# Sparse attention: softmax weights transposed as a rounded part and a rest

## The chip, the cores and the metric

The kernel runs on one NeuronCore of a Trainium2 chip. The metric is the device time of one execution in microseconds. The kernel before was run three times: 3642.68, 3643.70 and 3645.34 us, median 3643.7.

## The reference, cut to what matters

The model has two blocks. In its second layer stands a sparse attention over 16 + 512 tokens with 16 heads; a query attends to a chosen set of latent key rows:

```python
def block(qa, qi, wi, qpos):
    ...                       # index scores, the best keys of each query
    logits = (jnp.einsum("bqhr,bqkr->bqhk", qa, kv).astype(jnp.float32) * B_KV_RANK ** -0.5
              + jnp.swapaxes(bias, -1, -2))
    p = jax.nn.softmax(jnp.where(valid[:, :, None, :], logits, NEG_INF), axis=-1)
    o_lat = jnp.einsum("bqhk,bqkr->bqhr", p.astype(kv.dtype), kv)
    o = jnp.einsum("bqhr,hrd->bqhd", o_lat, w_uv)
```

All is float32. The change touches how the weights p get from query rows to key rows between the softmax and the product with the values.

## The kernel before

The program is one long chain of stages on one core, written engine by engine with semaphores; nothing is scheduled by a tool, so the order on each engine is the order in the code. The feed-forward stages (`fa_`, `fb_`, `fd_`, `ff_`) fill most of the time. Their matmuls are of type float32r, a reduced float32: an operand is written as a rounded part (`xh`, `wh`) and the rest (`xl`, `wl`), and three products are summed in PSUM (L371, L430). The sparse attention computes with plain float32 matmuls; the profile shows each of them as two records.

`dsa_stage` runs `latents` (projections, norms) and then `latent_heads`, the place of the change. `latent_heads` first makes the queries of all heads (L1602, weights fetched in three slots), their norms, and the index scores with the choice of keys on DVE. Then comes the head loop. A step g is one head `hd` and one query tile `t` of four, with 144, 272, 400 and 528 visible keys; there are 16 * 4 = 64 steps.

- PE: `turn(g)` (L1643) transposes the weights of step g, first the 16 meta keys (L1652, the data as a 128x16 stationary operand, the identity as 128 moving columns), then t + 1 blocks of 128x128 (L1654); `scores(g + 4)` (L1638) computes logits four steps ahead, since each tile has its own PSUM bank; `outputs(hd - 1)` (L1662, L1664) follows in the step t = 0. The last step of a head also waits for `mixed`, since its meta block goes to the bank of the outputs.
- DVE: `logit(g)` scales and adds the bias from PSUM (L1817), adds the mask and takes the maximum (L1820); then `weigh(g - 1)` takes the reciprocal of the denominator (L1827) and multiplies (L1829), in place in `b_work`.
- ACT: `spread(g)` copies the turned blocks to SBUF (L1745, L1748), then `exps(g + 3)` (L1735); `store` copies a head's output to `b_mix` (L1753).
- SP fetches: behind the last norm sum (L1576) it issues the first two of eight output weights (L1580), the others each behind a finished output product (L1698).

The buffers: `b_work` (`early`) holds queries, scratch and, later, logits and turned weights; the tile `b_vals` holds the values, and `l_q_all` the queries of all heads.

Of the kernel before, what the change touches and what calls it, by code (L numbers as in the profile page):

```python
# [15 lines left out]
P = 128  # L16
# [48 lines left out]
        "q_mm q_ev squared added_sq ssq_mm i_mm relued i_added v_mm v_ev u_mean u_root scored logits expd "  # L65
# [27 lines left out]
def build(nc, x_t, meta_t, mem_t, bias_onehot, dil_onehot, rel_bias, dil_table, gains, wi, wo, w_out,  # L93
# [3 lines left out]
    with top:  # L97
# [1211 lines left out]
        EARLY = IDX_COLS + 4 * TOK + 6 * SEQ + 2 * SEQ + 3 * 2 * RANK  # L1309

        def early_parts(early):

            at, parts = 0, []
            for cols, shape, names in ((4 * SEQ, "p (c t) -> p c t", {"c": 4}), (TOK, None, {}),
                                       (4 * TOK, "p (s t) -> p s t", {"s": 4}),
                                       (4 * SEQ, "p (s r t) -> p s r t", {"s": 2, "r": 2}),
                                       (2 * SEQ, "p (s t) -> p s t", {"s": 2}), (2 * SEQ, "p (k t) -> p k t", {"k": 2}),
                                       (6 * RANK, "p (s n) -> p s n", {"s": 3})):
                part = early[:, at:at + cols]
                parts.append(part.rearrange(shape, **names) if shape else part)  # L1320
                at += cols
            return parts

        def dsa_stage():
            with ExitStack() as st:
                mix = sb(st, "b_mix", [P, KC, SEQ])
                bw = sb(st, "b_bw", [P, HEADS, TOK])
                ckv = sb(st, "b_ckv", [P, 2, TOK])
                vals = sb(st, "b_vals", [P, QT, B_HEADS * 64])
                valm = sb(st, "b_valm", [META, B_HEADS * 64])  # L1330
                mb = sb(st, "b_mb", [P, QT, TOK])
                g_lat = sb(st, "b_g_lat", [P, 3, 2])
                early = sb(st, "b_work", [P, EARLY])
                widx = sb(st, "b_widx", [P, QT, IDX_HEADS])
                eps_q = sb(st, "b_eps_q", [P, QT])
                uv = mix[:, 0:4, :].rearrange("p k t -> p (k t)").rearrange("p (h n) -> p h n", h=B_HEADS)
                c_bw, uq0, uq1, uq2, uv_there = sems(st, "b_")
                uq_there = [uq0, uq1, uq2]
                with ExitStack() as s2:
                    latents(s2, ckv, g_lat, widx, eps_q, uv, bw, c_bw, early, uq_there, uv_there)  # L1340
                with ExitStack() as s2:
                    latent_heads(s2, ckv, vals, valm, g_lat, widx, eps_q, mb, mix, uv, bw, c_bw, early, uq_there, uv_there)

        def latents(st, ckv, g_lat, widx, eps_q, uv, bw, c_bw, early, uq_there, uv_there):
# [13 lines left out]
            qidx, kidx, _, _, _, qn, w_uq = early_parts(early)  # L1358
# [161 lines left out]
        def latent_heads(st, ckv, vals, valm, g_lat, widx, eps_q, mb, mix, uv, bw, c_bw, early, uq_there, uv_there):  # L1520

            q_all = sb(st, "l_q_all", [P, 2 * B_HEADS, SEQ])
            top8 = sb(st, "l_top8", [P, 8])
# [5 lines left out]
            qidx, kidx, act_r, sq, sq_sum, qn, w_uq = early_parts(early)  # L1529
# [4 lines left out]
            WO_AT = EARLY - 2 * KC * P  # L1534
            pt = early[:, PT_AT:PTM_AT].rearrange("p (u j q) -> p u j q", u=2, j=QT)
            ptm = early[:, PTM_AT:PTM_AT + 2 * SEQ].rearrange("p (u q) -> p u q", u=2)
            w_o = early[:, WO_AT:EARLY].rearrange("p (s n) -> p s n", s=2)
            (q_mm, q_ev, squared, added_sq, ssq_mm, i_mm, relued, i_added, v_mm, v_ev, u_mean, u_root, scored, logits,
# [31 lines left out]
            with nc.Block() as block:  # L1570
                @block.sync
                def _(sp):
                    for hd in range(3, B_HEADS):
                        sp.wait_ge(q_mm, 1 + hd - 2)
                        sp.dma_start(w_uq[:, hd % 3, :], b_uq[hd]).then_inc(uq_there[hd % 3], 16)
                    sp.wait_ge(ssq_mm, 1 + B_HEADS)  # L1576
                    for c in range(KC):
                        if c >= 2:
                            sp.wait_ge(o_mm, 1 + c - 1)
                        sp.dma_start(w_o[:, c % 2, :], w_out[1, c]).then_inc(wo_there[c % 2], 16)  # L1580
                    fetch_first(sp, 3)

                @block.gpsimd
                def _(pool):
                    for hd in range(B_HEADS):
# [8 lines left out]
                def _(pe):  # L1594
# [48 lines left out]
                    def turn(g):  # L1643
# [6 lines left out]
                        pd, bank = lg_of(g), T_BANK[g % 2]  # L1650
                        to = acc[0:META, bank, (t + 1) * P:(t + 2) * P] if t < NT - 1 else acc[0:META, O_BANK, 0:P]
                        pe.transpose(to, pd[:, 0:META], ident[:, :])  # L1652
                        for j in range(t + 1):
                            last = pe.transpose(acc[:, bank, j * P:(j + 1) * P], pd[:, META + j * P:META + (j + 1) * P],  # L1654
                                                ident[:, :])
# [26 lines left out]
                    pe.wait_ge(v_ev, 1 + len(v_jobs))  # L1682
                    for g in range(LAST):
# [92 lines left out]
                def _(dve):  # L1776
# [46 lines left out]
                    def weigh(g):  # L1823
                        lg = lg_of(g)
                        s = g % 8
                        dve.wait_ge(expd, 1 + g + 1)
                        dve.reciprocal(rden[:, s:s + 1], den[:, s:s + 1])  # L1827
                        dve.drain()
                        dve.tensor_scalar(lg, lg, rden[:, s:s + 1], None, ALU.mult).then_inc(weights, 1)  # L1829
# [1473 lines left out]
```

## Time and profile before

| | |
|---|---|
| median of three runs | 3643.7 us |
| profiled execution, its own time | 3643.14 us |
| its span | 3641.3 us, 51388 instructions |
| granted TensorE clock, mean | 0.984 of 2.4 GHz |
| PE busy | 3518.0 us (97%) |
| DVE busy | 1752.5 us (48%) |
| ACT busy | 1329.3 us (37%) |
| head loop, first to last turn | 1715.6 to 1866.8 us of the span |

How to read it: a busy PE means that some matmul record is open, not that the array is at its peak; successive records overlap, so the time that a matmul takes in a stream is the distance between two starts, not its length. PEld is the load of the stationary operand. Where the view merges records ("x3"), the length runs from the first start to the last end. The granted clock is 1.00 for 2.4 GHz and 0.50 for 1.2 GHz.

### The profile page before, as it was taken

The numbers are of one execution on the slowest core, as the hardware profiler recorded it, in microseconds if no ns is written. First come the engines' busy times: TensorE is split into PE (matmuls) and PEld (weight loads), VectorE is DVE, ScalarE is ACT, GpSimd is POOL, SyncE is SP. The second block draws the span as 40 slices with busy tenths as digits, with TensorE's granted clock in tenths as the row PEclk, the third lists the DMA queues.
The fourth block names the chain that finished last, engine by engine and source line by source line (L and its number), as shares of the span: only waits on it lengthen the run. The fifth ranks groups of instructions, "written<-read, shape, count | busy, mean of one in ns | idle before, by whom it ended". The sixth has DMA issues, their size and how long they took to land. (4 is left out here: it accounts for less than half of the span.)

```text
span 3641.3 us, 51388 instructions
## 1 busy us (share of the span) xinstructions
PE 3518.0 (97%) x20338; PEld 2956.1 (81%) x20338; DVE 1752.5 (48%) x2511; ACT 1329.3 (37%) x1840; POOL 596.1 (16%) x656
## 2 busy tenths in 40 slices
PE   8999999999999999988999999999989999899998
PEld 7999977799999999754547888888866677678886
DVE  5443377554434443266635443544269633554433
ACT  4332366443323332134524332333231244334421
POOL 0000122200000000011005755540032323320000
PEclk9999999899999999989999999999999999999999
DMA  5322411032222222300003223332234421322222
GB/s 171 136 85 88 142 52 48 21 108 86 81 88 106 82 89 83 136 24 27 1 29 110 101 108 121 130 117 86 87 128 142 148 64 53 132 100 104 94 93 79
DMA packets 124082, 334.91 MB, mean 92 GB/s; under 512 B 15192, under 2 KB 58456, under 8 KB 107957
## 3 DMA queue, kind: packets, MB, share of 16 engines
q1 hardware_dynamic: 120884, 324.90, 25.9%
q0 software_dynamic: 3072, 8.39, 0.6%
q8 instruction: 72, 1.18, 0.1%
q14 instruction: 54, 0.43, 0.0%
HBM read 316.36 MB, written 25.40 MB: 94 GB/s over the span
## 5 line engine op out<-in xcount | busy, mean ns | idle before, releaser
L371 PE MATMUL acc<-fb_xh,fb_wh 128*128 128x264 f32 x1408 | 287.7, 285 | 3.2 <-DVE fb_wl L550 3.2
L371 PE MATMUL acc<-fb_xl,fb_wh 128*128 128x264 f32 x1408 | 288.0, 286 | 0.0
L371 PE MATMUL acc<-fb_xh,fb_wl 128*128 128x264 f32 x1408 | 287.5, 286 | 0.0
L371 PE MATMUL acc<-fd_xh,fd_wh 128*128 128x512 f32 x704 | 275.4, 391 | 3.2 <-DVE fd_wl L550 3.2
L371 PE MATMUL acc<-fd_xl,fd_wh 128*128 128x512 f32 x704 | 274.4, 390 | 0.0
L371 PE MATMUL acc<-fd_xh,fd_wl 128*128 128x512 f32 x704 | 274.4, 390 | 0.0
L446 ACT ACTIVATE fb_wh<-fb_raw 128x2048 fp32r<-128x2048 f32 (+1 forms) x74 | 124.7, 1686 | 286.9 <-PE acc L430 173.8
L371 PEld LDWEIGHTS acc<-fb_xh,fb_wh 128*128 128x128 f32 x1408 | 219.9, 189 | 3.6 <-DVE fb_wl L550 3.5
L371 PEld LDWEIGHTS acc<-fb_xl,fb_wh 128*128 128x128 f32 x1408 | 219.2, 189 | 0.0
L371 PEld LDWEIGHTS acc<-fb_xh,fb_wl 128*128 128x128 f32 x1408 | 218.7, 189 | 0.0
L545 DVE TENSOR_TENSOR fb_wl<-fb_raw,fb_wh 128x2048 fp32r<-128x2048 f32 (+1 forms) x74 | 148.3, 2004 | 141.2 <-ACT fb_wh L446 140.3
L446 ACT ACTIVATE fd_wh<-fd_raw 128x2048 fp32r<-128x2048 f32 (+1 forms) x74 | 124.8, 1686 | 248.2 <-PE acc L430 158.0
L545 DVE TENSOR_TENSOR fd_wl<-fd_raw,fd_wh 128x2048 fp32r<-128x2048 f32 (+1 forms) x74 | 152.3, 2058 | 130.5 <-ACT fd_wh L446 129.4
L446 ACT ACT_TABLE_LOAD x60 | 77.0, 1283 | 298.8 <-PE acc L371 298.7
L1589 POOL TENSOR_TENSOR b_work<-b_work 128x512 f32<-128x512 f32 x16 | 20.7, 1295 | 949.5 <-ACT b_work L1717 949.5
L784 POOL TENSOR_TENSOR fa_wl<-fa_raw,fa_wh 128x1024 fp32r<-128x1024 f32 x30 | 71.1, 2375 | 633.0 <-ACT fa_wh L1026 633.0
L371 PEld LDWEIGHTS acc<-fd_xh,fd_wh 128*128 128x128 f32 x704 | 132.5, 188 | 31.7 <-DVE fd_wl L550 4.0
L371 PEld LDWEIGHTS acc<-fd_xl,fd_wh 128*128 128x128 f32 x704 | 132.5, 188 | 28.1 <-issue 0.5
L371 PEld LDWEIGHTS acc<-fd_xh,fd_wl 128*128 128x128 f32 x704 | 132.4, 188 | 27.7
L371 PE MATMUL acc<-fa_xh,fa_wh 128*128 128x264 f32 x704 | 144.3, 286 | 7.3 <-DVE fa_wl L550 7.3
L642 DVE SCALAR_TENSOR_TENSOR h<-acc,h 128x264 f32<-128x264 f32 (+1 forms) x72 | 35.1, 516 | 230.9 <-PE acc L430 230.9
L371 PE MATMUL acc<-fa_xl,fa_wh 128*128 128x264 f32 x704 | 144.4, 286 | 0.0
(555 smaller groups left out, 9141.1 us busy)
## 6 DMA issues: line engine op xcount, KB each, us to landing
fb_raw<-wi_dram SPq DMA_DIRECT2D x42, 1024.0 KB, 4.7
fd_raw<-wi_dram SPq DMA_DIRECT2D x42, 1024.0 KB, 4.8
fb_raw<-wo_dram SPq DMA_DIRECT2D x32, 704.0 KB, 4.0
fd_raw<-wo_dram SPq DMA_DIRECT2D x32, 704.0 KB, 4.1
fa_raw<-wi_dram SPq DMA_DIRECT2D x20, 1024.0 KB, 4.7
ff_raw<-wi_dram SPq DMA_DIRECT2D x20, 1024.0 KB, 4.7
fa_raw<-a_qkv_dram SPq DMA_DIRECT2D x24, 512.0 KB, 4.1
m_raw<-gate_w_dram SPq DMA_DIRECT2D x24, 512.0 KB, 3.4
```

The costliest lines, as they stand in the source:

```text
L371: last = pe.matmul(acc[:, up_base(p, b) + 2 * a + q, 0:w], x[:, k, a, :], part[:, k, t0:t0 + w], start=k == 0 and part is xh and x is wv, ...
L446: act.activation(wh[:, b, 0:n_], raw[:, b, 0:n_], ACT.Copy).then_inc(rounded, 1)
L545: dve.tensor_tensor(wl[:, b, 0:n_], raw[:, b, 0:n_], wh[:, b, 0:n_].bitcast(F32), ALU.subtract).then_inc(split, 1)
L642: last = dve.scalar_tensor_tensor(hv, acc[:, down_base(p) + 2 * (c % 2) + q, 0:w], 0.5, hv, ALU.mult, ALU.add)
L784: pool.tensor_tensor(wl[:, c % RING, :], raw[:, c % RING, :], wh[:, c % RING, :].bitcast(F32), ALU.subtract).then_inc(split, 1)
L1589: pool.tensor_tensor(sq_sum[:, hd % 2, :], sq[:, hd % 2, 0, :], sq[:, hd % 2, 1, :], ALU.add).then_inc(added_sq, 1)
```

## The change

`turn` no longer uses the transposing form on float32 data. `weigh` now writes two float32r tiles, `hi` (the product, rounded by its output type) and `lo` (the product again, less `hi`), into a new buffer `l_pd` with two slots, g mod 2. `turn` multiplies each block twice by an identity of type float32r, once for each part, and the bank sums them. POOL makes this identity once. Since `l_pd` has two slots, `weigh(g)` waits until `turn(g - 2)` is done. To make room, `early` gets smaller: the normed query latents move to `b_vals`, the three slots of query weights to `b_mix`, and the output weights to the first four planes of `l_q_all`, so that their loads wait until the scores of heads 0 and 1 are computed.

```diff
-        EARLY = IDX_COLS + 4 * TOK + 6 * SEQ + 2 * SEQ + 3 * 2 * RANK
+        EARLY = 2 * sum(keys for _, _, keys, _ in REAL_TILES) + 2 * QT * SEQ + 2 * SEQ
...
+                qn = vals[:, 0, :].rearrange("p (k t) -> p k t", k=2)
+                w_uq = mix[:, 4:7, :]
...
+            ident_r = sb(st, "l_ident", [P, P], F32R)
...
+            pd = sb(st, "l_pd", [P, 2, 2, TOK], F32R)
...
-            w_o = early[:, WO_AT:EARLY].rearrange("p (s n) -> p s n", s=2)
+            w_o = q_all[:, 0:4, :].rearrange("p c t -> p (c t)").rearrange("p (s n) -> p s n", s=2)
...
-                    sp.wait_ge(ssq_mm, 1 + B_HEADS)
+                    sp.wait_ge(scored, 1 + 2 * NT)
...
+                    pool.tensor_copy(ident_r[:, :], ident[:, :]).then_inc(ident_on, 1)
...
-                        pd, bank = lg_of(g), T_BANK[g % 2]
+                        bank, keys = T_BANK[g % 2], WIDTHS[t]
                         to = acc[0:META, bank, (t + 1) * P:(t + 2) * P] if t < NT - 1 else acc[0:META, O_BANK, 0:P]
-                        pe.transpose(to, pd[:, 0:META], ident[:, :])
+                        for r in range(2):
+                            pe.matmul(to, pd[:, g % 2, r, 0:META], ident_r[:, :], start=r == 0, stop=r == 1)
                         for j in range(t + 1):
-                            last = pe.transpose(acc[:, bank, j * P:(j + 1) * P], pd[:, META + j * P:META + (j + 1) * P],
-                                                ident[:, :])
+                            for r in range(2):
+                                last = pe.matmul(acc[:, bank, j * P:(j + 1) * P],
+                                                 pd[:, g % 2, r, META + j * P:META + (j + 1) * P], ident_r[:, :],
+                                                 start=r == 0, stop=r == 1)
                         last.then_inc(turned, 1)
...
+                    pe.wait_ge(ident_on, 2)
...
+                        hi, lo = (pd[:, g % 2, r, 0:WIDTHS[STEPS_[g][1]]] for r in range(2))
                         dve.reciprocal(rden[:, s:s + 1], den[:, s:s + 1])
                         dve.drain()
-                        dve.tensor_scalar(lg, lg, rden[:, s:s + 1], None, ALU.mult).then_inc(weights, 1)
+                        if g >= 2:
+                            dve.wait_ge(turned, 1 + g - 1)
+                        dve.tensor_scalar(hi, lg, rden[:, s:s + 1], None, ALU.mult)
+                        dve.drain()
+                        dve.scalar_tensor_tensor(lo, lg, rden[:, s:s + 1], hi.bitcast(F32), ALU.mult,
+                                                 ALU.subtract).then_inc(weights, 1)
```

On PE, in the head loop from the last three steps of one head into the next, the order before (each row is line, operation, output and inputs, output size and count):

```order
L1652 MATMUL acc<-ident,b_work 16x128
L1654 MATMUL acc<-ident,b_work 128x128 x2
L1638 MATMUL acc<-b_ckv,l_q_all 128x272 x2
L1652 MATMUL acc<-ident,b_work 16x128
L1654 MATMUL acc<-ident,b_work 128x128 x3
L1638 MATMUL acc<-b_ckv,l_q_all 128x400 x2
L1652 MATMUL acc<-ident,b_work 16x128
L1654 MATMUL acc<-ident,b_work 128x128 x4
L1638 MATMUL acc<-b_ckv,l_q_all 128x512 x2
```

And the same place now (turns are L1656 and L1659, scores L1641):

```order
L1656 MATMUL acc<-l_ident,l_pd 16x128 x2
L1659 MATMUL acc<-l_ident,l_pd 128x128 x4
L1641 MATMUL acc<-b_ckv,l_q_all 128x272 x2
L1656 MATMUL acc<-l_ident,l_pd 16x128 x2
L1659 MATMUL acc<-l_ident,l_pd 128x128 x6
L1641 MATMUL acc<-b_ckv,l_q_all 128x400 x2
L1656 MATMUL acc<-l_ident,l_pd 16x128 x2
L1659 MATMUL acc<-l_ident,l_pd 128x128 x8
L1641 MATMUL acc<-b_ckv,l_q_all 128x512 x2
```

Nothing changes place on PE; each turning instruction became two.

On DVE, at the start of the head loop (steps 0 and 1), before:

```order
L1827 RECIPROCAL l_rden<-l_den 128x1
L1829 TENSOR_SCALAR b_work<-b_work,l_rden 128x144
L1817 SCALAR_TENSOR_TENSOR b_work<-acc,l_rq,b_bw 128x400
L1820 ISA b_work,l_nmx<-b_work,b_mb 128x400
L1820 ISA l_nmx 128x1
L1827 RECIPROCAL l_rden<-l_den 128x1
L1829 TENSOR_SCALAR b_work<-b_work,l_rden 128x272
```

And now (logits are L1824 and L1827, the weights L1835 to L1841):

```order
L1835 RECIPROCAL l_rden<-l_den 128x1
L1839 TENSOR_SCALAR l_pd<-b_work,l_rden 128x144
L1841 SCALAR_TENSOR_TENSOR l_pd<-b_work,l_rden,l_pd 128x144
L1824 SCALAR_TENSOR_TENSOR b_work<-acc,l_rq,b_bw 128x400
L1827 ISA b_work,l_nmx<-b_work,b_mb 128x400
L1827 ISA l_nmx 128x1
L1835 RECIPROCAL l_rden<-l_den 128x1
L1839 TENSOR_SCALAR l_pd<-b_work,l_rden 128x272
L1841 SCALAR_TENSOR_TENSOR l_pd<-b_work,l_rden,l_pd 128x272
```

One operation per step is added behind the multiplication, and the next logit stands behind it.

## Rows read from the trace of the kernel before

**Rows 1.** Page, part 1: busy time of each engine and share of the span.

```profile
PE 3518.0 (97%) x20338; PEld 2956.1 (81%) x20338; DVE 1752.5 (48%) x2511; ACT 1329.3 (37%) x1840; POOL 596.1 (16%) x656
```

**Rows 2.** Windows around the head loop: busy us, granted clock, DMA share, GB/s.

```profile
1715.60:1719.00 3.40, 3.24 (x12) 2.69 (x13) 3.02 (x10) 1.25 (x5) 0.00 (x0) 0.50 0.02 5
...
1780.00:1820.00 40.00, 40.00 (x181) 22.92 (x180) 25.34 (x84) 22.35 (x73) 0.00 (x0) 1.00 0.00 1
```

**Rows 3.** Timeline, PE: start us, length us, engine, line; one head apart.

```profile
1794.05 1.07 PE L1662 MATMUL acc<-b_work,b_valm 16*64 16x512 f32 x2
...
1803.81 1.07 PE L1662 MATMUL acc<-b_work,b_valm 16*64 16x512 f32 x2
```

**Rows 4.** Timeline, PE: one turn of three full blocks.

```profile
1798.59 0.27 PE L1652 MATMUL acc<-ident,b_work 128*16 128x128 f32 x1
1798.70 0.49 PE L1654 MATMUL acc<-ident,b_work 128*128 128x128 f32 x3
1799.03 1.51 PE L1638 MATMUL acc<-b_ckv,l_q_all 128*128 128x400 f32 x4
```

**Rows 5.** Timeline: records of few columns behind full weight loads.

```profile
1690.32 1.03 PE L1609 MATMUL acc<-ones,b_work 128*128 128x1 f32 x8
...
1792.88 0.41 PEld L1638 LDWEIGHTS acc<-b_ckv,l_q_all 128*128 128x128 f32 x3 [0.24 <-issue]
```

**Rows 6.** Timeline, PE: float32r matmuls of 264 and of 512 columns.

```profile
1200.39 0.41 PE L371 MATMUL acc<-fb_xh,fb_wh 128*128 128x264 f32 x2
1200.63 0.41 PE L371 MATMUL acc<-fb_xl,fb_wh 128*128 128x264 f32 x2
...
2299.87 0.39 PE L371 MATMUL acc<-fd_xh,fd_wh 128*128 128x512 f32 x1
...
2300.10 0.39 PE L371 MATMUL acc<-fd_xl,fd_wh 128*128 128x512 f32 x1
```

**Rows 7.** One line's instructions: float32r weight loads, ns min/median/max.

```profile
L371 PEld LDWEIGHTS acc<-fb_xh,fb_wh x1408: 187/188/333, 738.3 to 1386.1; 128*128 128x128 f32 x176
```

**Rows 8.** Groups by form, PE: the float32r matmul of fewest columns.

```profile
L2495 PE MATMUL acc<-d_mh,m_wh 128*128 128x256 f32 x64 | 18.6, 290 | 0.0
```

**Rows 9.** Timeline, PE: the two records of a float32 matmul of 128 columns.

```profile
1797.03 0.38 PE L1664 MATMUL acc<-b_work,b_vals 128*64 128x128 f32 x2
```

**Rows 10.** Timeline, DVE: logit steps at the loop's start, unbroken until 1722.10.

```profile
1715.40 0.63 DVE L1817 SCALAR_TENSOR_TENSOR b_work<-acc,l_rq,b_bw 128x400 f32<-128x400 f32 x1
...
1722.50 0.63 DVE L1817 SCALAR_TENSOR_TENSOR b_work<-acc,l_rq,b_bw 128x400 f32<-128x400 f32 x1 [0.40 <-PE acc L1638]
```

**Rows 11.** Groups by form, DVE: times of one; the three-operand form in SBUF.

```profile
L1829 DVE TENSOR_SCALAR b_work<-b_work,l_rden 128x528 f32<-128x528 f32 x16 | 7.9, 496 | 1.2
...
L1192 DVE SCALAR_TENSOR_TENSOR a_pd<-a_lg,a_rden,a_pd 128x528 f32<-128x528 f32 x8 | 6.1, 768 | 0.7
...
L1192 DVE SCALAR_TENSOR_TENSOR a_pd<-a_lg,a_rden,a_pd 128x400 f32<-128x400 f32 x8 | 5.1, 635 | 0.7
...
L1192 DVE SCALAR_TENSOR_TENSOR a_pd<-a_lg,a_rden,a_pd 128x272 f32<-128x272 f32 x8 | 4.0, 502 | 0.7 <-issue 0.2
...
L1192 DVE SCALAR_TENSOR_TENSOR a_pd<-a_lg,a_rden,a_pd 128x144 f32<-128x144 f32 x8 | 3.0, 370 | 0.6
```

**Rows 12.** Waits in the head loop: us in total, times, longest.

```profile
DVE b_work L1817 <- PE acc L1638: 41.0, 44, 1.8
```

**Rows 13.** Timeline: first and second turn of the loop, and the last.

```profile
1715.64 0.37 PE L1652 MATMUL acc<-ident,b_work 128*16 128x128 f32 x1 [3.17 <-DVE b_work L1829]
...
1717.30 0.09 PEld L1652 LDWEIGHTS acc<-ident,b_work 128*16 128x16 f32 x1 [0.47 <-DVE b_work L1829]
...
1866.85 0.27 PE L1652 MATMUL acc<-ident,b_work 128*16 128x128 f32 x1 [0.75 <-ACT b_mix L1753]
```

**Rows 14.** One line's instructions: the loads of the output weights.

```profile
L1580 SPq DMA_DIRECT2D b_work<-w_out_dram x8: 327/328/434, 1691.4 to 1913.2; - x8
...
DMA to landing us min/median/max: 3.3/3.5/4.3
```

More of the change, by code:

```diff
@@ L64 @@
     "l_": (
-        "q_mm q_ev squared added_sq ssq_mm i_mm relued i_added v_mm v_ev u_mean u_root scored logits expd "
+        "ident_on q_mm q_ev squared added_sq ssq_mm i_mm relued i_added v_mm v_ev u_mean u_root scored logits expd "
         "weights turned pt_ready pv_mm mixed wo0 wo1 o_mm o_added"),
@@ L1316, in early_parts @@
                                        (4 * SEQ, "p (s r t) -> p s r t", {"s": 2, "r": 2}),
-                                       (2 * SEQ, "p (s t) -> p s t", {"s": 2}), (2 * SEQ, "p (k t) -> p k t", {"k": 2}),
-                                       (6 * RANK, "p (s n) -> p s n", {"s": 3})):
+                                       (2 * SEQ, "p (s t) -> p s t", {"s": 2})):
                 part = early[:, at:at + cols]
@@ L1339, in dsa_stage, with latents @@
                 with ExitStack() as s2:
-                    latents(s2, ckv, g_lat, widx, eps_q, uv, bw, c_bw, early, uq_there, uv_there)
+                    latents(s2, ckv, g_lat, widx, eps_q, uv, qn, w_uq, bw, c_bw, early, uq_there, uv_there)
                 with ExitStack() as s2:
-                    latent_heads(s2, ckv, vals, valm, g_lat, widx, eps_q, mb, mix, uv, bw, c_bw, early, uq_there, uv_there)
-        def latents(st, ckv, g_lat, widx, eps_q, uv, bw, c_bw, early, uq_there, uv_there):
+                    latent_heads(s2, ckv, vals, valm, g_lat, widx, eps_q, mb, mix, uv, qn, w_uq, bw, c_bw, early, uq_there, uv_there)
+        def latents(st, ckv, g_lat, widx, eps_q, uv, qn, w_uq, bw, c_bw, early, uq_there, uv_there):
             xn = sb(st, "b_xn", [P, KC, TOK])
@@ L1357, in latents @@
             s_q = sb(st, "b_s_q", [P, QT])
-            qidx, kidx, _, _, _, qn, w_uq = early_parts(early)
+            qidx, kidx, _, _, _ = early_parts(early)
             (there_g, there_i, there_cq, there_kv, there_q, sq_a, sq_d, summed, rooted, normed, idx_mm, cq_mm,
@@ L1518, in _, with latent_heads @@
                     last.then_inc(ckv_on, 1)
-        def latent_heads(st, ckv, vals, valm, g_lat, widx, eps_q, mb, mix, uv, bw, c_bw, early, uq_there, uv_there):
+        def latent_heads(st, ckv, vals, valm, g_lat, widx, eps_q, mb, mix, uv, qn, w_uq, bw, c_bw, early, uq_there, uv_there):
             q_all = sb(st, "l_q_all", [P, 2 * B_HEADS, SEQ])
+            ident_r = sb(st, "l_ident", [P, P], F32R)
             top8 = sb(st, "l_top8", [P, 8])
@@ L1528, in latent_heads @@
             rden = sb(st, "l_rden", [P, 8])
-            qidx, kidx, act_r, sq, sq_sum, qn, w_uq = early_parts(early)
+            qidx, kidx, act_r, sq, sq_sum = early_parts(early)
+            pd = sb(st, "l_pd", [P, 2, 2, TOK], F32R)
             WIDTHS = [keys for _, _, keys, _ in REAL_TILES]
@@ L1533, in latent_heads @@
             PTM_AT = PT_AT + 2 * QT * SEQ
-            WO_AT = EARLY - 2 * KC * P
             pt = early[:, PT_AT:PTM_AT].rearrange("p (u j q) -> p u j q", u=2, j=QT)
             ptm = early[:, PTM_AT:PTM_AT + 2 * SEQ].rearrange("p (u q) -> p u q", u=2)
-            w_o = early[:, WO_AT:EARLY].rearrange("p (s n) -> p s n", s=2)
-            (q_mm, q_ev, squared, added_sq, ssq_mm, i_mm, relued, i_added, v_mm, v_ev, u_mean, u_root, scored, logits,
+            w_o = q_all[:, 0:4, :].rearrange("p c t -> p (c t)").rearrange("p (s n) -> p s n", s=2)
+            (ident_on, q_mm, q_ev, squared, added_sq, ssq_mm, i_mm, relued, i_added, v_mm, v_ev, u_mean, u_root, scored, logits,
              expd, weights, turned, pt_ready, pv_mm, mixed, wo0, wo1, o_mm, o_added) = sems(st, "l_")
```

## The prediction

> **What bounds the kernel now.** I read the busy shares first: PE is busy for 97% of the span, DVE for 48% [rows 1]. That says little of one stage, so I then read the windows around the head loop, where the change acts: in its steady part PE is busy for 40.00 of 40 us at full clock, DVE for 25.3, ACT for 22.4, and hardly a byte moves [rows 2]. Then two starts of the same matmul one head apart: 1794.05 and 1803.81, so a head takes 9.76 us [rows 3]. DVE waits for the scores of PE for 41.0 us in 44 places of the loop [rows 12]. PE sets the pace, and what is added to PE's stream in the loop is added to the time, as long as DVE keeps up.
>
> In a stream the price of a matmul is the distance between starts. In a turn of one meta block and three full blocks the starts are 1798.59, 1798.70 and, for what follows, 1799.03: 0.11 for the meta block and 0.33 / 3 = 0.11 for each full one [rows 4]. A turn of tile t has t + 2 such intervals, the last reaching to the next instruction's first record. A head has 2 + 3 + 4 + 5 = 14, so 1.54 of its 9.76 us are turning.
>
> **What sets 0.11 us.** It could be 128 columns streaming at two cycles each, or the load of the next 128 stationary columns. The trace tells them apart. Eight norm-sum records stream a single column each behind a full load, and take 1.03 us together: at most 0.13 each [rows 5]. Three loads for score records of 16 columns span 0.41 us, with 0.19 as one's own length [rows 5, 7], so they start (0.41 - 0.19) / 2 = 0.11 apart. So one full float32 load per 0.11 us is the floor, whatever streams behind it. The trace has no float32r load that is dense enough to show its floor: with 264 columns the starts are 0.24 us apart for two, 0.12 each, and with 512 columns 0.23 [rows 6]. Two things follow from these: float32r streams one column per cycle (0.107 and 0.213 us at 2.4 GHz), with some 0.013 us on top. The load's own length is 187 to 188 ns in float32r [rows 7], which is also what the loads in rows 5 show. I take the floor to be the same, 0.11.
>
> **The change part by part, PE.** Each turn has twice the instructions, with a load each. The intervals of the new turn: from the first meta pass to the second, where the next load has only 16 columns, so that the streaming decides: 128 / 2.4 = 0.053 us and the 0.013, 0.066; from there 2(t + 1) intervals that each end in a full load, 0.11; and the last one to the scores' load, 0.11 as before. Over a head: 4 * 0.066 + 20 * 0.11 + 4 * 0.11 = 2.90 us against 1.54, which is 1.36 more. Sixteen heads: 21.8 us. Bounds of the one unseen price, the interval of a full float32r load behind a pass of 128 columns: from above 0.22 us, two float32 records of 128 columns, which start 0.38 - 0.27 = 0.11 apart [rows 4, 9]; from below 0.053 us, the streaming alone. I take 0.11, since the nearest rows, those with few columns, lie there. With 0.1225 as in rows 6 the loop would take 4 us more, and with 0.11 for the meta pass 2.8 more.
>
> **DVE.** The new operation reads SBUF and has three operands. The same form took 370, 502, 635 and 768 ns at these widths, and the drain ahead of it costs as L1829's idle, 1.2 us in 16 or 0.075 [rows 11]. Per head: 2.28 + 0.30 = 2.58 us. DVE's present need per head I read where it does not wait: from 1715.40 to 1722.50 - 0.40 = 1722.10 it does four steps, one of each width, in 6.70 us [rows 10]. So it will need 9.3 us against PE's 9.76 + 1.36 = 11.1. If the multiplication with a float32r output fell to the pace of the three-operand form (768 instead of 496 ns at the widest, at most 0.27 in each step), 10.4. Covered in both cases; the cover is 0.7 to 1.8 us per head, and beyond it each microsecond costs 16.
>
> **The new wait.** `weigh(g)` waits for `turn(g - 2)`, and behind it on DVE stand `logit(g + 2)` and all else. From the end of `turn(g - 2)` to the start of `turn(g)` PE has two blocks of scores and a turn to do; the 400-column block alone lasts 1.51 us [rows 4], and the multiplication with the rest needs at most 0.50 + 0.08 + 0.77 = 1.35. No wait for PE comes of it in the steady part. ACT's work is as before, and its share is the smallest of the three.
>
> **Start and end of the loop.** The first turn waits 3.17 us for the first weights, and the second turn's load waits again for DVE [rows 13]. There DVE is on the path: up to the second turn come 0.37 + 0.08 and 0.50 + 0.08, 1.0 us, of which the sum above holds 0.2 for the first turn. The clock stands at 0.50 there [rows 2]; if it stays so over the next two turns, their added passes, 0.29 + 0.40 us, take about twice that. Together 1.5 us. At the end the last turn waits for ACT's store for 0.75 us [rows 13], which hides a part of the passes added just before it, and the last weights come 0.85 later; I count nothing.
>
> **The rest.** POOL copies 128x128 once, long before it is needed: nothing. The first two output weights are issued some 30 us later than at 1691.4, and land in 3.5 us [rows 14], still over 140 us before they are used. Query weights and latents only move. Nothing.
>
> The sum: 21.8 + 1.5 = 23.3 us on the profiled execution's 3643.14 gives 3666.4; the median of the runs lies 0.6 above it, so 3667.0.
>
> **The rivals.** First, the load of a float32r block is shorter than 0.11 and hides under the pass. Then 24 intervals per head fall to 0.066 and four stay: 1.58 + 0.44 = 2.02, 0.48 more than now, 7.7 us in sixteen heads, with the start 9.2: 3653. For it speaks that no row shows a dense float32r load; against it that its length is the float32 one. If then the multiplication fell to the slower pace, DVE's 10.4 would bind over PE's 10.2, 3 us more. The Trainium skill ("TensorE: Matmul & The Clock Gate", Weight-path perf modes — Fast Weight Load (FWL) and DoubleRow) says that fast weight load is on for 128 weights if the input type is not FP32, and measured about twice the speed. Whether float32r counts as FP32 the page does not say; by that rule, if it does not, the load would be some 54 ns as an estimate from that page and the time this rival's. Rows 7, where a float32r load lasts as long as a float32 one, speak against it.
>
> Second, on the other side, not slower: the transposing form costs two cycles a column, as many as two float32r passes of one cycle each, and neither loads nor the 0.013 us count. All 28 intervals are 0.053: 1.49 instead of 1.54, which gives back 0.8 us and leaves the start's 1.5: 3644. It decides from a mean interval of (1.54 + 5.8 / 16) / 28 = 0.068 us downward, since a measurement of this kernel can tell about 0.2%, 7.3 us, from no change. It needs the one-column records of rows 5 to be an exception.
>
> Third, a float32r pass under 256 columns costs as much as the float32 matmul of its size, two records, 0.22 us. The float32r matmul of fewest columns in the trace has 256 [rows 8], so no row excludes it; against it stands that float32r matmuls show one record each [rows 6]. Then 28 * 0.22 = 6.16 against 1.54, 4.6 per head, 74 and 1.5: 3719.
>
> Fourth, DVE binds, by slower writes of the new type than any bound above: at 12 us per head 36 + 1.5, 3681.
>
> **How the numbers follow.** The forecast gets 0.72, its own range 3664 to 3675 (0.053 for the meta pass at one end, 0.1225 and 0.11 at the other). The first rival 0.10, the second 0.04, the third 0.11, the fourth 0.03. The range must take in the first rival and the fourth: 3652 to 3682, which leaves out the second and the third. Slower by over 0.2%: forecast, third, fourth and nearly all of the first, 0.94; same 0.05; faster 0.01.
>
> **What would show it.** Starts of the output matmul one head apart: 11.1 us if I am right, 10.2 for the first rival, 9.7 for the second, 14.4 for the third. Starts of full turning passes 0.11 apart, each with its load; the distance of the two meta passes near 0.066. PE still busy for 40 of 40 us, DVE for about 30 of 40 and waiting for scores less than now. The new operation at 768 ns for 528 columns, and the multiplication near 496. I am wrong if the distance of the full passes is not near 0.11, or if PE has gaps in the loop that end at DVE's weights.

## The result and the profile after

The changed kernel takes 3671.3 us (median of four runs, 3670.94 to 3673.33) against 3644.5 us of the kernel before. The ratio of the runs is 1.0078, 95% interval 1.0065 to 1.0090. Over five more runs, with the kernel before beside them, it was 1.0072 (1.0058 to 1.0085): slower by 26 to 28 us, where 23.3 were forecast.

First the page of the changed kernel, its span and its busy shares:

```profile
span 3669.7 us, 51967 instructions
PE 3545.9 (97%) x20562; PEld 2981.7 (81%) x20562; DVE 1789.5 (49%) x2575; ACT 1329.4 (36%) x1840; POOL 592.8 (16%) x657
```

The shares are those of [rows 1] to a point, and tell nothing of the stage. The windows do (columns as in [rows 2]: PE, PEld, DVE, ACT and POOL busy us, granted clock, DMA share, GB/s). Steady loop, its start, and what follows its end:

```profile
1719.00:1722.00 3.00, 2.63 (x12) 2.25 (x12) 2.73 (x9) 1.06 (x5) 0.00 (x0) 0.50 0.02 5
...
1780.00:1820.00 40.00, 40.00 (x211) 25.34 (x210) 30.02 (x87) 19.29 (x63) 0.00 (x0) 1.00 0.00 1
...
1894.00:1896.00 2.00, 2.00 (x5) 0.74 (x5) 0.00 (x0) 0.00 (x0) 0.00 (x0) 0.72 0.00 0
1896.00:1898.00 2.00, 2.00 (x7) 0.87 (x5) 0.00 (x0) 0.02 (x1) 0.00 (x0) 0.50 0.00 0
```

PE is busy for 40.00 of 40 us as before, DVE for 30.0 where it was 25.3, which is 8.4 us of a head's 11.15. At the start the clock is 0.50, as in [rows 2]. In the last pair, behind the last turn, the clock stands at 0.72 and 0.50, where the trace of before has 1.00.

Next the timeline of PE across one head, which answers to [rows 3]:

```profile
1797.00 1.07 PE L1668 MATMUL acc<-b_work,b_valm 16*64 16x512 f32 x2
...
1803.72 0.59 PE L1656 MATMUL acc<-l_ident,l_pd 128*16 128x128 f32 x2
1804.15 1.05 PE L1659 MATMUL acc<-l_ident,l_pd 128*128 128x128 f32 x8
...
1807.18 0.28 PE L1656 MATMUL acc<-l_ident,l_pd 128*16 128x128 f32 x2
1807.29 0.38 PE L1659 MATMUL acc<-l_ident,l_pd 128*128 128x128 f32 x2
...
1808.15 1.07 PE L1668 MATMUL acc<-b_work,b_valm 16*64 16x512 f32 x2
```

From one output product to the next it is 1808.15 - 1797.00 = 11.15 us; it was 9.76, and 11.1 was forecast. Eight full passes span 1.05 us and two span 0.38, so the starts are (1.05 - 0.38) / 6 = 0.112 us apart. (In two of four turns, as at 1803.72, the record of the first meta pass starts already 0.03 us behind the start of the last scores record, so its own start can't be read there.) Another turn shows the meta passes and what follows, answering to [rows 4]:

```profile
1800.30 0.29 PE L1656 MATMUL acc<-l_ident,l_pd 128*16 128x128 f32 x2
...
1800.43 0.61 PE L1659 MATMUL acc<-l_ident,l_pd 128*128 128x128 f32 x4
...
1802.64 1.56 PE L1641 MATMUL acc<-b_ckv,l_q_all 128*128 128x400 f32 x4
```

From the first meta pass to the first full pass it is 0.13 us for two intervals; over the loop the median from the second meta pass to the first full one is 0.060, near the forecast 0.066. But the first full pass also starts within 0.06 to 0.07 us of the pass before it and not 0.11. On the other side the four records of the scores behind a turn span 1.56 us where they spanned 1.51 [rows 4]: what the start of a turn gains is given back at its end, 0.05 us each, four times in a head. Both belong to one and the same thing, the price of a full load, which shows one record late. The first scores record behind the turn is 551 ns long and those behind it 499, and the surplus of 0.052 is the load's 0.112 less the 0.060 that the last pass streams. So a full pass and the scores behind a turn each cost 0.112 and only the second meta pass 0.060: 24 * 0.112 + 4 * 0.060 = 2.93 us in a head against 1.54, which is 1.39 more. The kernel with half the columns, below, tells this from a cost of changing the type.

DVE's new operation and its multiplication, by form (times as in [rows 11]):

```profile
L1841 DVE SCALAR_TENSOR_TENSOR l_pd<-b_work,l_rden,l_pd 128x528 fp32r<-128x528 f32 x16 | 12.3, 769 | 1.2
...
L1839 DVE TENSOR_SCALAR l_pd<-b_work,l_rden 128x528 fp32r<-128x528 f32 x16 | 7.9, 495 | 17.1 <-PE acc L1659 17.1
```

They take 769 and 495 ns for 528 columns, as the same forms in the rows before, so the float32r output costs nothing. DVE's waits in the loop:

```profile
DVE l_pd L1839 <- PE acc L1659: 17.1, 15, 1.4
...
DVE b_work L1824 <- PE acc L1641: 9.6, 14, 0.7
```

It waits for scores for 9.6 us instead of 41.0 [rows 12], and for the turn two steps back for 17.1. Both are waits of an engine that is ahead. The start and the end of the loop, which answer to [rows 13]:

```profile
1718.24 0.37 PE L1656 MATMUL acc<-l_ident,l_pd 128*16 128x128 f32 x2 [3.61 <-DVE l_pd L1841]
...
1891.10 0.29 PE L1656 MATMUL acc<-l_ident,l_pd 128*16 128x128 f32 x2 [0.64 <-DVE l_pd L1841]
...
1893.12 1.07 PE L1668 MATMUL acc<-b_work,b_valm 16*64 16x512 f32 x2 [0.83 <-ACT b_work L1755]
```

The first turn waits 3.61 us instead of 3.17, 0.44 more for the first rest. The last turn now waits for DVE's rest and no longer for ACT's store, 0.64 us instead of 0.75, and the output product behind it waits 0.83 us for ACT. The loads of the output weights, as in [rows 14]:

```profile
L1582 SPq DMA_DIRECT2D l_q_all<-w_out_dram x8: 327/328/434, 1729.3 to 1939.6; - x8
DMA to landing us min/median/max: 3.4/3.5/4.5
```

The first is issued 38 us later and lands 165 us before its use at 1897.9.

**A ledger of the stage.** The table takes starts of the same matmuls in both traces. The values' matmuls, the last ahead of the loop, end their starts at 1711.9 and 1714.0:

```profile
L1627 PE MATMUL acc<-b_mix,b_ckv x40: 592/592/1061, 1691.3 to 1711.9; 128*128 128x512 f32 x32, 128*16 128x512 f32 x8
```

```profile
L1630 PE MATMUL acc<-b_mix,b_ckv x40: 592/592/697, 1696.8 to 1714.0; 128*128 128x512 f32 x32, 128*16 128x512 f32 x8
```

| stretch | before, us | after, us | more | forecast |
|---|---|---|---|---|
| last matmul of the values to the first output product (turns 0 to 4) | 13.8 | 16.1 | 2.3 | 3.0 |
| first to last output product (turns 5 to 63) | 142.7 | 163.0 | 20.3 | 20.3 |
| last output product to the first matmul with the output weights | 3.3 | 4.8 | 1.5 | 0 |
| from there to the next stage | 58.4 | 58.6 | 0.2 | 0 |
| sum | 218.2 | 242.5 | 24.3 | 23.3 |

The profiled executions differ by more, 3671.51 - 3643.14 = 28.4 us. What lies outside the ledger is asked by the first experiment and by the second trace of the changed kernel. Taken off the spans, the ledger leaves 3423.1 and 3424.7 us in the first two traces of before, and 3427.3 and 3422.9 in the two of the changed kernel.

### The profile page after: what moved, and what is told of

The parts are those of the page before. It is cut to its first block and busy times, and to the rows that moved or that the text cites. A ratio compares the mean times of both kernels' runs of the same rounds, so it can differ in the third digit from the quotient of the medians.

```text
span 3669.7 us, 51967 instructions
## 1 busy us (share of the span) xinstructions
PE 3545.9 (97%) x20562; PEld 2981.7 (81%) x20562; DVE 1789.5 (49%) x2575; ACT 1329.4 (36%) x1840; POOL 592.8 (16%) x657
## 5 line engine op out<-in xcount | busy, mean ns | idle before, releaser
L371 PEld LDWEIGHTS acc<-fb_xl,fb_wh 128*128 128x128 f32 x1408 | 218.5, 188 | 0.0
L371 PE MATMUL acc<-fa_xh,fa_wl 128*128 128x264 f32 x704 | 144.0, 286 | 0.0
```

The source lines that it names most:

```text
L371: last = pe.matmul(acc[:, up_base(p, b) + 2 * a + q, 0:w], x[:, k, a, :], part[:, k, t0:t0 + w], start=k == 0 and part is xh and x is wv, ...
```

## The experiments

**The kernel before once more.**

> The kernel before once more, for a second trace of it. The trace of the changed kernel stands 4.7 us later than that of before already ahead of the sparse attention (first matmul of the feed-forward stage before it at 743.0 against 738.3), in code that the change doesn't touch, and the values of the sparse attention took 3.3 us less. Theory (these are differences from one execution to the next): this trace differs from the first one of the same kernel by some us in those same stages, with the head loop at 9.76 us per head as before. Rival (they come with the changed program): the stages stand within 0.5 us of the first trace. Ratio to before 1.000 in both.

There was no edit. The ratio is 0.9999 (0.9989 to 1.0009). One line's instructions, the first matmuls of the feed-forward stage ahead of the attention (first and last start behind the comma), in the first trace of before, in this one, in that of the changed kernel, and in that of the one-pass kernel below:

```profile
L371 PE MATMUL acc<-fb_xh,fb_wh x1408: 279/285/587, 738.3 to 1386.3; 128*128 128x264 f32 x176
```

```profile
L371 PE MATMUL acc<-fb_xh,fb_wh x1408: 279/285/479, 741.4 to 1389.3; 128*128 128x264 f32 x176
```

```profile
L371 PE MATMUL acc<-fb_xh,fb_wh x1408: 279/285/479, 743.0 to 1390.9; 128*128 128x264 f32 x176
```

```profile
L371 PE MATMUL acc<-fb_xh,fb_wh x1408: 279/285/479, 734.8 to 1382.8; 128*128 128x264 f32 x176
```

The same code starts anywhere from 734.8 to 743.0 us, and the same program differs by 3.1 between two executions. The theory holds: offsets ahead of the attention are no effect of the change. The loop stood at 9.76 us per head, and the ledger's sum at 218.7. Within it two stretches differ. Up to the first output product it is 12.7 us and not 13.8, since the clock rose again 3.0 us behind the first turn instead of 5.7. And from the last output product to the output weights it is 4.9 us and not 3.3, at a low clock:

```profile
1868.00:1870.00 2.00, 2.00 (x5) 0.33 (x4) 0.00 (x0) 0.00 (x0) 0.00 (x0) 0.84 0.00 0
1870.00:1872.00 2.00, 2.00 (x5) 0.90 (x4) 0.00 (x0) 0.00 (x0) 0.00 (x0) 0.50 0.00 0
```

The question that this raises is taken up at the end.

**The layout alone.**

> The change's layout alone: latents, query weights and output weights moved, their loads later, the identity copied by POOL, but one float32 transposing pass per block and the weights in place as before. Theory (the layout costs nothing): 3644, ratio 1.000, head 9.76 us. Rival (the moved buffers or the later loads cost a part of the 28 us between the two profiled executions that the head loop doesn't explain, about 4 us): 3648, ratio 1.001.

```diff
-                        for r in range(2):
-                            pe.matmul(to, pd[:, g % 2, r, 0:META], ident_r[:, :], start=r == 0, stop=r == 1)
+                        pe.transpose(to, lg_[:, 0:META], ident[:, :])
...
-                        dve.tensor_scalar(hi, lg, rden[:, s:s + 1], None, ALU.mult)
...
+                        dve.tensor_scalar(lg, lg, rden[:, s:s + 1], None, ALU.mult).then_inc(weights, 1)
```

Median 3644.19, ratio 1.0004 (0.9995 to 1.0014), ledger's sum 218.2 as before. The layout costs nothing that can be measured.

**DVE's part alone.**

> DVE does all the work of the changed kernel and waits for the turn two steps back, but PE turns only the rounded part, in the transposing form as before; the rest is left out of the output. Theory (all of the loop's cost is PE's passes, DVE and its new wait cost only at the start of the loop): head 9.76 us, about 1 us over the layout alone, 3645. Rival (DVE's longer step and its wait hold PE up): head over 9.9 us, 3 us or more over the layout alone, and PE idle in the loop behind DVE's weights.

```diff
-                        for r in range(2):
-                            pe.matmul(to, pd[:, g % 2, r, 0:META], ident_r[:, :], start=r == 0, stop=r == 1)
+                        hi_ = pd[:, g % 2, 0, :].bitcast(F32)
+                        pe.transpose(to, hi_[:, 0:META], ident[:, :])
```

(The full blocks likewise.) Median 3644.79, ratio 1.0004 (0.9994 to 1.0013); the ledger's sum is 219.7, 1.5 more than before: 1.2 at the start, and 0.25 in the last head, where the last turn waits 0.99 us for DVE's rest instead of 0.75 for ACT. Two output products one head apart on PE's timeline:

```profile
1786.51 1.07 PE L1666 MATMUL acc<-b_work,b_valm 16*64 16x512 f32 x2
...
1796.27 1.07 PE L1666 MATMUL acc<-b_work,b_valm 16*64 16x512 f32 x2
```

9.76 us: DVE's longer step and its wait for the turn two steps back cost nothing in the steady loop. The rival falls. Behind the last turn the clock stays up:

```profile
1872.00:1874.00 2.00, 2.00 (x8) 0.88 (x7) 0.00 (x0) 0.00 (x0) 0.00 (x0) 1.00 0.00 0
```

**One float32r pass.**

> The changed kernel with one float32r pass per block, that of the rounded part; the rest is computed by DVE but left out of the output. Theory (a full weight load sets 0.11 us per full pass in float32r as in the transposing form, and only the meta pass is shorter): head 9.62 us (1.40 instead of 1.54 us of turning), 3644. Rival (the stream of the pass sets it, 0.066 us, and the second pass costs 0.11 only since something else goes with a pair): head 9.34 us, 3639.

```diff
-                        for r in range(2):
-                            pe.matmul(to, pd[:, g % 2, r, 0:META], ident_r[:, :], start=r == 0, stop=r == 1)
+                        for r in range(1):
+                            pe.matmul(to, pd[:, g % 2, r, 0:META], ident_r[:, :], start=r == 0, stop=True)
```

Median 3647.63 where 3644 was expected, ratio 1.0017 (1.0007 to 1.0026). PE's timeline over one head:

```profile
1790.42 1.07 PE L1668 MATMUL acc<-b_work,b_valm 16*64 16x512 f32 x2
...
1796.83 0.61 PE L1659 MATMUL acc<-l_ident,l_pd 128*128 128x128 f32 x4
...
1799.46 0.28 PE L1659 MATMUL acc<-l_ident,l_pd 128*128 128x128 f32 x1
...
1800.21 1.07 PE L1668 MATMUL acc<-b_work,b_valm 16*64 16x512 f32 x2
```

A head takes 9.79 us, neither the 9.62 of the theory nor the 9.34 of the rival. The interval of full passes is (0.61 - 0.28) / 3 = 0.11, as the theory says; what its 9.62 missed is that behind the single meta pass comes a full load, so no interval is short and all 14 cost 0.112, 1.57 us instead of 1.54. The second pass then costs 11.15 - 9.79 = 1.36 us per head, and that is four times 0.060 and ten times 0.112. So the loop's cost is the number of passes, and nothing that goes with a pair.

The stage is 5.0 us longer than in the kernel with the same DVE work and the transposing form (224.6 against 219.7), though the loop is only 0.03 us per head longer; the medians of the two kernels differ by 2.8, of times that spread over 8 to 10 us. The ledger shows where: 16.5 us up to the first output product (15.1 there), 6.0 us behind the last (3.3 there). The windows behind the last turn:

```profile
1867.00:1869.00 2.00, 2.00 (x3) 0.46 (x2) 0.00 (x0) 0.00 (x0) 0.00 (x0) 0.50 0.00 0
1869.00:1871.00 2.00, 2.00 (x6) 0.92 (x4) 0.00 (x0) 0.00 (x0) 0.00 (x0) 0.50 0.00 0
```

The clock is at 0.50 in both, and at 0.63 and 0.67 in the windows next to them; there the output product runs at half speed. The two programs differ only in the form of the turning passes, but their traces also in the moment at which the loop ends; which of the two counts is asked at the end.

**Half the columns, and half the load.**

> The changed kernel, but each full turning pass streams only 64 of its 128 identity columns; loads are as they were, and half of each turned block is left out of the output. Theory (the load of 128 stationary columns sets the interval): full passes stay 0.11 us apart and a head 11.15 us, time as the changed kernel. Rival (streaming sets it): the intervals between full passes, 16 per head, fall by 0.027 to 0.055 us, a head to 10.7 or less, 7 us or more off the time.

```diff
-                                last = pe.matmul(acc[:, bank, j * P:(j + 1) * P],
-                                                 pd[:, g % 2, r, META + j * P:META + (j + 1) * P], ident_r[:, :],
+                                last = pe.matmul(acc[:, bank, j * P:j * P + 64],
+                                                 pd[:, g % 2, r, META + j * P:META + (j + 1) * P], ident_r[:, 0:64],
```

Median 3673.68, ratio 1.0084 (1.0067 to 1.0101), that of the changed kernel or more. PE over one head:

```profile
1794.76 1.07 PE L1668 MATMUL acc<-b_work,b_valm 16*64 16x512 f32 x2
...
1800.36 1.59 PE L1641 MATMUL acc<-b_ckv,l_q_all 128*128 128x400 f32 x4
...
1801.90 1.03 PE L1659 MATMUL acc<-l_ident,l_pd 128*128 128x64 f32 x8
...
1805.05 0.35 PE L1659 MATMUL acc<-l_ident,l_pd 128*128 128x64 f32 x2
...
1805.90 1.07 PE L1668 MATMUL acc<-b_work,b_valm 16*64 16x512 f32 x2
```

> The changed kernel, but each full turning pass loads only 64 stationary columns and writes 64 rows; it streams 128 columns as before, and half of each turned block is left out of the output. Theory (the load sets the interval, at 0.11 us per 128 columns): with half the load the stream of 0.066 us decides, 16 intervals per head fall by 0.046 us, a head to 10.4 us, 12 us off the time of the changed kernel. Rival (each float32r pass of 128 columns costs 0.11 us whatever is loaded): head 11.15 us, no gain.

```diff
-                                last = pe.matmul(acc[:, bank, j * P:(j + 1) * P],
-                                                 pd[:, g % 2, r, META + j * P:META + (j + 1) * P], ident_r[:, :],
+                                last = pe.matmul(acc[0:64, bank, j * P:(j + 1) * P],
+                                                 pd[:, g % 2, r, META + j * P:META + j * P + 64], ident_r[:, :],
```

Median 3655.48, ratio 1.0029 (1.0017 to 1.0040). PE over one head:

```profile
1788.31 1.07 PE L1668 MATMUL acc<-b_work,b_valm 16*64 16x512 f32 x2
...
1793.42 1.56 PE L1641 MATMUL acc<-b_ckv,l_q_all 128*128 128x400 f32 x4
...
1794.94 0.65 PE L1659 MATMUL acc<-l_ident,l_pd 128*64 128x128 f32 x8
...
1797.68 0.28 PE L1659 MATMUL acc<-l_ident,l_pd 128*64 128x128 f32 x2
...
1798.44 1.07 PE L1668 MATMUL acc<-b_work,b_valm 16*64 16x512 f32 x2
```

With half the columns to stream the full passes stay (1.03 - 0.35) / 6 = 0.113 us apart and a head takes 11.14 us. With half the columns to load they are (0.65 - 0.28) / 6 = 0.062 apart and a head takes 10.13. So in a full float32r pass the load of 128 stationary columns sets the pace, 0.112 us, and the stream of 128 moving columns hides in it; with 64 to load the stream sets it, 0.062. The 20 full passes of a head fall by 0.051 each, 1.02 us, which is the whole difference to 11.15; I had expected 16 intervals to fall by 0.046.

The scores behind a turn, four records of 400 columns, show where the surplus of 0.05 us comes from. They span 1.51 us behind transposing passes, 1.56 behind float32r passes of 128 columns (with 128 or 64 columns loaded), and 1.59 behind those of 64 columns. The change of type is the same in the last three, so it does not set the surplus. What does, by this reading, is the scores' own load of 0.112 us less what the last pass covers of it: 0.060 with 128 columns, and some 0.03 with 64 (half of it, an estimate), which leaves 0.05 and 0.08.

The half-column kernel's loop is the changed kernel's, yet its ledger's sum is 248.7, 6.2 more. That lies at the ends: 20.9 us up to the first output product instead of 16.1, 6.2 behind the last instead of 4.8. Its windows from the first turn on, first and last of five in a row:

```profile
1711.00:1714.00 3.00, 2.42 (x12) 2.11 (x13) 2.73 (x8) 1.03 (x4) 0.00 (x0) 0.50 0.02 5
...
1723.00:1726.00 3.00, 3.00 (x4) 1.04 (x4) 0.64 (x2) 1.13 (x4) 0.00 (x0) 0.50 0.00 0
```

All five stand at 0.50, 15 us in all, and the clock rises only in the window behind them (0.81); in the changed kernel the window from 1724 to 1726, 6 us behind its first turn, is back at 0.95. Why it stays low longer here the runs do not show.

**The start of the loop.** Both traces show PE idle ahead of the first turn and then turning at the low clock. ACT loads its exponential table only behind the last eviction of the values, and the first exponential only then; in the trace of before:

```profile
1712.51 0.60 ACT L1730 ACTIVATE b_vals<-acc 128x512 f32<-128x512 f32 x1 [1.12 <-PE acc L1627]
1713.12 1.28 ACT L1735 ACT_TABLE_LOAD   x1
```

> The kernel before, with the first three exponentials of the head loop issued by ACT among the evictions of the values (behind the fifth, seventh and ninth) instead of behind them all. Theory (PE's idle 3.2 us ahead of the first turn comes from ACT's table load and first exponential behind the evictions, and the granted clock of 0.5 after it from that idle time): the first turn follows the values' last eviction at once, the clock stays at 1.0, some 5 us less, 3639. Rival (the exponentials delay the evictions, PE waits for a free bank among the values instead): no gain, PE idle among the values' matmuls by as much.

```diff
                     for n in range(len(v_jobs)):
                         take_values(n)
-                    for g in range(3):
-                        exps(g)
+                        if n in (4, 6, 8):
+                            exps(n // 2 - 2)
```

Median 3635.71, ratio 0.9976 (0.9967 to 0.9986): faster than both kernels. The first pass on PE and the window around it:

```profile
1712.89 0.28 PE L1652 MATMUL acc<-ident,b_work 128*16 128x128 f32 x1 [0.69 <-ACT b_vals L1730]
```

```profile
1712.00:1716.00 4.00, 3.31 (x21) 2.53 (x21) 2.31 (x8) 3.07 (x11) 0.00 (x0) 1.00 0.00 0
```

PE waits 0.69 us instead of 3.17, for the last eviction, and the clock is 1.00. The ledger's sum is 212.8, 5.4 under before, all of it up to the first output product: 8.5 us instead of 13.8. Of this 2.5 is the shorter wait; the other 2.9 came with the full clock. The values are not held up: their matmuls take 16.9 us from first start to last, no more than in any other trace (16.9 to 20.6), so the rival falls. The runs say 8.7 (5 to 12), which holds the 5.4.

> The changed kernel with the same move of the first three exponentials. Theory: the first weights in two parts are then ready before the values end, so the 0.45 us of the first rest and the dearer passes at the low clock go too: some 6 us less than the changed kernel, 3665. Rival (the exponentials delay the evictions): no gain.

The same edit in the changed kernel: median 3662.48, ratio to before 1.0048 (1.0031 to 1.0064), ledger's sum 236.4, which is 6.1 under the changed kernel; up to the first output product 10.0 us instead of 16.1. The 5.0 us behind the last one stay, since the low clock there stays.

**The changed kernel once more.**

> The changed kernel once more, with more rounds and a second trace. From the end of the values to the feed-forward stage behind the attention its trace is 24.1 us longer than that of before, but the two profiled executions differ by 28.4. Theory (the change costs 24 us, the rest is how executions differ in stages that it doesn't touch): ratio near 1.0067, that stretch again 24 us longer, a head 11.15 us, the clock again low for some us behind the last turn. Rival (some 4 us of cost lie outside that stretch): ratio 1.0078 or more.

Median 3670.20, ratio 1.0072 (1.0058 to 1.0085). The ledger's sum is 242.6 us, the head 11.15, the clock 0.53 and 0.61 behind the last turn. And the first matmuls of the feed-forward stage ahead of the attention, where the first trace of the changed kernel had 743.0:

```profile
L371 PE MATMUL acc<-fb_xh,fb_wh x1408: 279/285/479, 736.4 to 1384.4; 128*128 128x264 f32 x176
```

The two traces of the same program differ by 6.6 us there, and their spans, 3669.7 and 3665.5, by 4.2. The interval of the ratio holds both 1.0067 and 1.0078, so the timing alone does not decide; the ledgers do for the stage, at 24 us in both traces. The medians differ by 26.8 us both times. Whether the 2 to 3 us between that and the ledgers are lost elsewhere is not settled.

**The clock behind the last turn.** It was low in all six traces with float32r turns, and in one of five with transposing turns. Three more traces of kernels shown above, on another chip, were to tell whether the form has to do with it.

> The kernel before, a third trace. Behind the last turn the granted clock fell to 0.50 for some us in all six traces with float32r turns, and in one of five with transposing turns (the second trace of this kernel, 4.9 us from the last output product to the next matmuls instead of 3.3). Theory (the form of the turning passes makes it likelier): 3.3 us and clock 1.00 here. Rival (it comes and goes from one execution to the next, whatever the form): about as often 4.8 us and clock 0.50.

> The kernel with DVE's part alone (transposing turns), a second trace, for the same question. Theory: 3.3 us from the last output product to the next matmuls, clock 1.00. Rival: 4.8 us or more and clock 0.50 about as often.

> The kernel with the layout alone (transposing turns), a second trace, for the same question. Theory: 3.3 us and clock 1.00. Rival: 4.8 us or more and clock 0.50 about as often.

The single times were 3643.76, 3644.33 and 3645.11 us. All three show 3.3 us from the last output product to the next matmuls and a clock of 1.00; the window of the first of them that ends with those matmuls:

```profile
1870.00:1872.00 2.00, 2.00 (x9) 1.00 (x8) 0.00 (x0) 0.19 (x1) 0.00 (x0) 1.00 0.00 0
```

So it is seven of eight with transposing turns at 3.3 us, and six of six with float32r turns at 4.6 to 6.2. That looks like the form, but these counts do not show it, since the two groups differ in something else: when the end of the loop comes. In each of the fourteen traces the moments at which the granted clock changes lie on an even grid in time. In the seven traces in which the clock stayed up, the last output product starts in the first quarter of a step of this grid (six traces) or 0.02 us ahead of its start (one). In the seven in which it fell, it starts between 45% and 94% of a step, the exception with transposing turns among them (54%). The two traces of before show it with nothing else changed: PE waits 0.75 and 0.83 us at the end in both, but from the rise of the clock at the loop's start to the last output product it is 147.0 us where the clock stayed up and 148.6 where it fell. So the moment separates all fourteen traces, and the form only thirteen. This was read from the traces afterwards and no run tested it. No trace has float32r turns with an early end or transposing turns with a very late one, so whether the form adds anything stays open.

The ledger's sums, 218.5, 219.6 and 218.2, repeat the earlier ones of the same kernels to 0.3 us (before: 218.2, 218.7 with the low clock), so DVE's part costs 1.3 to 1.5 us, nearly all at the start.

## Why the prediction was right, point by point

**PE sets the pace and the passes are added to it.** Right. The loop grew by 20.3 us where its steady part was forecast at 20.3, and DVE's work alone left it at 9.76. That the two agree to the tenth is luck: a head grew by 1.39 instead of 1.36, and the last head, whose turns have no scores of a later head between them, by only 0.97.

**The load of 128 stationary columns sets 0.11 us in float32r too.** Right, and then shown by both sides: half the columns changed nothing, half the load took a head from 11.15 to 10.13 us. With it falls the first rival and, with it, the reading that a float32r load could be a fast one: by that rule of the Trainium skill ("TensorE: Matmul & The Clock Gate", Weight-path perf modes — Fast Weight Load (FWL) and DoubleRow), if float32r did not count as FP32, the full passes would have been near 0.066, and they are 0.112. The second rival (no load counts) falls with the same rows, the third (0.22 us under 256 columns) by the 0.112 itself. The fourth needed DVE at 12 us per head; it was busy for 30.0 of 40, or 8.4 per head.

**"From there 2(t + 1) intervals that each end in a full load, 0.11; and the last one to the scores' load, 0.11 as before".** Right in its count. The records seem to say otherwise, since the first full pass starts 0.06 us behind the last meta pass and the scores behind a turn take 0.05 us more than before, but that is the same 0.112 shown one record late. Two sizes were a little off: a full interval is 0.112, not 0.11, and a meta interval 0.060, not 0.066. The 0.013 us on top of the streaming, from which the 0.066 came, were worked out with a slip: 0.107 us is 256 columns, and 264 take 0.110. Net, a head grew by 1.39 instead of 1.36.

**"I count nothing" for the end of the loop.** This step failed. The added passes there are indeed nearly covered, but the clock fell to 0.50 behind the last turn and the last output product took 1.5 us more. Six traces of six with float32r turns show it, at 1.3 to 2.9 us over the 3.3 of before, and one of eight with transposing turns. What separates all of them is when the loop ends against the moments at which the clock can change, and a loop that is longer or shorter ends at another such moment. So these 1.5 us came with the change but may be the luck of its length, and the kernel before paid 1.6 of them once too. That the form of the passes has a part in it is not shown.

**The start, 1.5 us.** The rest's 0.37 + 0.08 before the first turn were 0.44. But the stretch up to the first output product grew by 2.3 instead of 3.0, since the added passes were counted double for the low clock. The clock rose 5.7 us behind the first turn before and 6.0 us behind it in the changed kernel: the low stretch did not grow with the added work, so more of the scores ran at the full clock. Its length is not fixed, though: it was 3.0 us in the second trace of before and 16 in the half-column kernel.

**The rest of the edit costs nothing.** Right: 1.0004 for the layout alone.

Together 24.3 against 23.3 in the stage. Of the 28.4 between the first two profiled executions the other 4 lie outside it, where traces of one and the same program also differ by 4 us (3427.3 and 3422.9 in the changed kernel). The medians' 26.8 leave 2 to 3 us that nothing here assigns.

## What to carry to other kernels

In a stream of small matmuls, each with its own stationary operand, count the stationary columns first: here 128 of them cost 0.11 us in float32r as in float32, so a type with half the streaming brings nothing, and splitting an operand that has to be stationary doubles the price. Price a stage by the distance between starts of the same matmul one loop turn apart, and not by single records, which show a load one record late; the forecast of 1.36 us met 1.39. And look at what ACT does between two phases: moving a table load and three exponentials into its slack was worth 5.4 us in the stage of a kernel whose PE was busy for 97% of the time.

## What the runs showed of the hardware that was not expected

- A full load that the pass before it does not cover lengthens the record of its own matmul and not the distance to the record before. The first full pass starts 0.06 us behind the last meta pass, and the scores record behind the turn is longer by 0.052 us, or by 0.083 where the passes stream 64 columns. Full behind full the distance is 0.112.
- The granted clock fell to 0.50 behind the last turn in seven of fourteen traces, six of them with float32r turns. The moment at which the loop ends, against the even grid on which the clock changes, separates the two groups without exception.
- The granted clock of 0.50 at the loop's start lasted as long with twice the turning passes as without (6.0 and 5.7 us behind the first turn), so work added there cost what it costs at the full clock.
- ACT's table load for the exponentials took 1.28 us, and with the exponentials set among copies from PSUM it still came only once.
- The three-operand form on DVE takes as long with a float32r output as with a float32 one (769 and 768 ns for 528 columns), and so does the multiplication by a scalar (495 and 496).
